# Paged latent attention of a decoder step: cache pages held as 64 partitions with turned rotary keys, and another order of TensorE's steps

## The reference

```python
past_ckv = cache_ckv[page_table].reshape(bd, -1, MLA_KV_RANK)   # 256 wide
past_kr = cache_krope[page_table].reshape(bd, -1, MLA_ROPE)     # 64 wide
s = (einsum('bqhr,bkr->bhqk', q_abs, ckv) + einsum('bqhd,bkd->bhqk', q_rope, kr)) * scale
s = where(k_pos <= q_pos, s, -inf)
o = einsum('bhqk,bkr->bqhr', softmax(s), ckv)
```

## Time and profile before

| what | value |
|---|---|
| time of three runs, median (lowest to highest) | 1618.31 us (1614.09 to 1619.07) |
| span of the profiled execution | 1614.3 us |
| TensorE busy (matmul, weight load) | 1531.1 us (95%), 1364.3 us (85%) |
| DVE, ACT, POOL busy | 821.2, 508.0, 674.4 us |
| first page transposes to last values | about 948 to 1122 us |

### The profile page before, as it was taken

One profiled execution on the slowest core, in us unless ns is written; L12 is line 12 of the kernel. 1 busy time (PEld: TensorE's weight loads), 2 busy tenths in 40 slices (PEclk: granted clock), 3 DMA queues, 4 the chain that ended last, 5 costly groups with the idle time before them and its releaser, 6 DMA issues.

```text
span 1614.3 us, 31112 instructions
## 1 busy us (share of the span) xinstructions
PE 1531.1 (95%) x11688; PEld 1364.3 (85%) x11688; DVE 821.2 (51%) x1212; ACT 508.0 (31%) x864; POOL 674.4 (42%) x558
## 2 busy tenths in 40 slices
PE   7999999979999999998899999999979999999996
PEld 7999645969999999997796556665969999999996
DVE  4721375476565663224647654443476665563224
ACT  5322340243222223113421444443243222223211
POOL 3343200346665564344332024441346665564333
PEclk9999997979999999998999999999989999999998
DMA  4222203212222223223121059982212222223221
GB/s 150 80 79 81 116 14 136 95 35 91 80 89 91 84 85 108 89 89 133 54 88 56 1 160 286 286 260 68 76 35 91 82 87 91 88 81 108 90 93 57
DMA packets 56215, 159.89 MB, mean 99 GB/s; under 512 B 7793, under 2 KB 26226, under 8 KB 54850
## 3 DMA queue, kind: packets, MB, share of 16 engines
q1 hardware_dynamic: 49986, 137.77, 25.7%
q0 software_dynamic: 6144, 20.98, 4.3%
HBM read 150.68 MB, written 8.05 MB: 98 GB/s over the span
## 4 chain that ended last, share of the span: by engine, by line
PE 84%; DVE 7%; issue 5%; ACT 2%; POOL 2%; POOLq 0%; ACTq 0%; DVEq 0%
PE lin L1510 61%; PE lin L1898 3%; PE px L1974 2%; PE px L1938 2%; DVE tb L1155 2%; POOL w_l L518 1%; PE lin L1869 1%; PE px L1886 1%; PE px L1942 1%; PE px L1906 1%; PE lin L1868 1%; DVE sq L1205 1%; DVE xg_l L979 1%; PE px L1575 1%; PE lin L1851 1%
## 5 line engine op out<-in xcount | busy, mean ns | idle before, releaser
L518 POOL TENSOR_TENSOR w_l<-w_raw,w_h 128x1024 fp32r<-128x1024 f32 (+1 forms) x142 | 384.7, 2710 | 380.9 <-ACT w_h L611 263.1
L1510 PE MATMUL lin<-xg_h,w_h 128*128 128x272 f32 x2112 | 459.3, 296 | 40.9 <-DVE xg_l L979 30.7
L1510 PE MATMUL lin<-xg_l,w_h 128*128 128x272 f32 x2112 | 447.4, 289 | 0.0
L1510 PE MATMUL lin<-xg_h,w_l 128*128 128x272 f32 x2112 | 446.8, 289 | 0.0
L1510 PEld LDWEIGHTS lin<-xg_h,w_h 128*128 128x128 f32 x2112 | 337.6, 190 | 51.0 <-DVE xg_l L979 24.8
L1510 PEld LDWEIGHTS lin<-xg_l,w_h 128*128 128x128 f32 x2112 | 340.1, 190 | 0.3
L1510 PEld LDWEIGHTS lin<-xg_h,w_l 128*128 128x128 f32 x2112 | 336.9, 190 | 0.0
L618 ACT ACTIVATE w_h<-w_raw 128x1024 fp32r<-128x1024 f32 (+1 forms) x104 | 117.3, 1128 | 233.3 <-PE lin L1510 233.3
L611 ACT ACTIVATE w_h<-w_raw 128x1024 fp32r<-128x1024 f32 (+2 forms) x71 | 77.9, 1099 | 241.5 <-PE lin L1510 223.4
L513 POOL TENSOR_TENSOR w_l<-w_raw,w_h 128x1024 fp32r<-128x1024 f32 (+2 forms) x33 | 83.9, 2543 | 166.3 <-ACT w_h L611 166.3
L1510 PE MATMUL lin<-a_h,w_h 128*128 128x272 f32 x704 | 150.4, 290 | 0.0
(11 more groups left out here) (307 smaller groups left out, 1978.7 us busy)
## 6 DMA issues: line engine op xcount, KB each, us to landing
w_raw<-w SPq DMA_DIRECT2D x139, 512.0 KB, 3.7
w_raw<-w SPq DMA_DIRECT2D x32, 704.0 KB, 4.0
pages<-cache SPq DMA_DIRECT2D x128, 160.0 KB, 3.7
pages<-cache POOLq DMA_DIRECT2D x128, 160.0 KB, 3.7
St<-state SPq DMA_DIRECT2D x4, 1024.0 KB, 7.7
gla_s<-St SPq DMA_DIRECT2D x4, 1024.0 KB, 3.9
w_raw<-w SPq DMA_DIRECT2D x4, 576.0 KB, 3.7
x<-x_t SPq DMA_DIRECT2D x4, 544.0 KB, 6.3
```

What stands on the lines that cost most here:

```text
L518: g.tensor_tensor(w_l[:, p % 2, 0:n], w_raw[:, p % 2, 0:n], w_h[:, p % 2, 0:n].bitcast(F32), ALU.subtract).then_inc(w_lo, 1)
L1510: last = mm(lin[:, 2 * out_set + half, 0:HALF], w[:, slot, (w0 + k) * P:(w0 + k + 1) * P], v[:, ch, half * HALF:(half + 1) * HALF], start= ...
```

## The change

A page in HBM is now 64 rows of 640 floats: row p holds the latent keys p and p + 64 (2 x 256) and then row p of the page's transposed rotary keys (128). A DMA writes 64 rows: SP always writes partitions 0 to 63, GpSimd 64 to 127, each with two of a group's four pages. So two pages share the 128 partitions, and their rotary keys need no transposes. The rotary scores multiply all 128 rows with `qz`, a query of which either the upper or the lower 64 rows are zero: eight matmuls of 256 columns (four runs of 64) for four of 512. There are 12 buffers instead of 14 (three of a unit's size): groups 0 to 3 wait for the prompt scores, 4 to 11 for the end of the prompt attention, later ones for the group 12 earlier. TensorE's order is groups 0 to 3, probabilities of u - 1, scores of u, values of u - 1; ACT and DVE follow it. The bytes per page stay 160 KB. The core of the diff:

```diff
@@ -210,20 +211,17 @@
...
-        qrs = at("qrs", Z + 41216, [P, NSEQ, 32])
...
+        qz = at("qz", Z + 41216, [P, 2, NSEQ, 32])
...
-        kr_t = at("kr_t", Z + 25600, [P, 2, SEQ])
...
+        pages = [at(f"pages{k}", o, [P, 8, PROW]) for k, o in enumerate((Z, Z + 67584, Z + 67584 + 4 * GROUP))]
...
@@ -313,44 +312,44 @@
...
-        def latent(g, j, lo=0, hi=KVR):
-            start = j * ROW + (ROPE if j % 2 else 0)
-            return pages[g % len(pages)][:, start + lo:start + hi]
-        def rotary_keys(g, pair):
-            return pages[g % len(pages)][:, 2 * pair * ROW + KVR:2 * pair * ROW + KVR + 2 * ROPE]
+        def latent(g, q4, lo=0, hi=KVR):
...
+        def rotary_keys(u, q4):
...
+            by_group = pages[u % len(pages)][:].rearrange("p (k e) c -> p k e c", e=2)
+            return by_group[:, :, par, 2 * KVR + 64 * key_half:2 * KVR + 64 * key_half + 64]
...
-        def load_pages(eng, which, ready):
...
+        def load_pages(eng, half, ready):
             eng.wait_ge(ids_in, 16)
-            eng.wait_ge(qa_ps, 1)
+            rows = slice(64 * half, 64 * half + 64)
             for g in range(4 * UNITS):
-                k = g % len(pages)
-                if g == 1:
+                k = g % SLOTS
+                if g == 0:
                     eng.wait_ge(sc_ps, H_M * TILES)
-                    eng.wait_ge(qr_done, 4)
-                elif g == 9:
+                    eng.wait_ge(qr_done, 6)
+                elif g == 4:
                     eng.wait_ge(ml_done, H_M)
...
-                elif g >= len(pages):
-                    eng.wait_ge(pvg_ps, g - len(pages) + 1)
-                for j in which:
-                    page = eng.value_load(page_ids[0:1, 4 * g + j:4 * g + j + 1], min_val=0, max_val=io["n_pool"] - 1)
-                    cols = slice(0, ROW) if j % 2 else slice(ROPE, ROPE + ROW)
-                    eng.dma_start(pages[k][:, j * ROW:(j + 1) * ROW], io["cache"][page, :, cols]).then_inc(ready[k], 16)
+                elif g >= SLOTS:
+                    eng.wait_ge(pvg_ps, g - SLOTS + 1)
+                for par in range(2):
+                    at_ = 4 * g + 2 * par + half
+                    page = eng.value_load(page_ids[0:1, at_:at_ + 1], min_val=0, max_val=io["n_pool"] - 1)
+                    eng.dma_start(pages[k // 4][rows, 2 * (k % 4) + par, :], io["cache"][page]).then_inc(ready[k], 16)
...
@@ -890,10 +889,6 @@
...
                 fn(k_t[:, :, 0, (g % 4) * P:(g % 4 + 1) * P], k_bank(g, 0).rearrange("p (j t) -> p j t", j=4), ACT.Copy).then_inc(ta_done, 1)
-                if g % 2:
-                    act.wait_ge(t_ps, turned(g, 3))
-                    fn(kr_t[:, :, (g % 4 - 1) * P:(g % 4 + 1) * P].rearrange("p j (e t) -> p e j t", e=2),
-                       r_bank.rearrange("p (e j t) -> p e j t", e=2, j=2), ACT.Copy).then_inc(tr_done, 1)
...
@@ -917,11 +912,10 @@
...
                     page_probs(unit_ - 1)
-                pages_turned(4 * unit_ + 1)
-                pages_turned(4 * unit_ + 2)
+                for kk in range(1, 4):
+                    pages_turned(4 * unit_ + kk)
                 if unit_:
...
-                pages_turned(4 * unit_ + 3)
             page_probs(UNITS - 1)
@@ -1367,8 +1361,9 @@
...
                 for to in range(2):
+                    v.memset(qz[ROPE * to:ROPE * to + ROPE, 1 - to], 0.0).then_inc(qr_done, 1)
                     for odd in range(2):
-                        v.tensor_copy(qrs[ROPE * to:ROPE * to + ROPE].rearrange("p b (j e t) -> p j e b t", j=4, t=TS)[:, :, odd],
+                        v.tensor_copy(qz[ROPE * to:ROPE * to + ROPE, to].rearrange("p b (j e t) -> p j e b t", j=4, t=TS)[:, :, odd],
                                       q[ROPE * odd:ROPE * odd + ROPE, 8:12, SEQ:NT].rearrange("p j (b t) -> p j b t", t=TS)).then_inc(qr_done, 1)
@@ -1431,14 +1426,13 @@
...
             for unit_ in range(UNITS):
-                for kk in range(3):
+                for kk in range(4):
                     pages_turned(4 * unit_ + kk)
...
                     new_probs_turned(unit_ - 1)
-                pages_turned(4 * unit_ + 3)
+                page_maxima(unit_)
                 if unit_:
                     page_outputs(unit_ - 1)
-                page_maxima(unit_)
             new_probs_turned(UNITS - 1)
@@ -1889,22 +1883,14 @@
             def turn_group(g):
-                for ready in (pg_ready, pg_odd):
-                    pe.wait_ge(ready[g % len(pages)], 32 * (g // len(pages) + 1))
+                for ready in (pg_low, pg_high):
+                    pe.wait_ge(ready[g % SLOTS], 32 * (g // SLOTS + 1))
                 for r in range(KC):
...
                         pe.wait_ge(ta_done if r == 0 else tv_done, g - 1)
...
                     last.then_inc(t_ps, 1)
-                if g % 2 == 0:
-                    return
-                if g > 1:
-                    pe.wait_ge(tr_done, g // 2)
-                for e in range(2):
-                    for j in range(2):
-                        last = nc.tensor.transpose(r_bank[:, (2 * e + j) * P:(2 * e + j + 1) * P], rotary_keys(g - 1 + e, j), ident[:])
-                last.then_inc(t_ps, 1)
...
@@ -1915,9 +1901,6 @@
...
-                if n == NM - 1:
-                    pe.wait_ge(pe_done, NM - 1)
-                    turn_group(0)
...
@@ -1932,26 +1915,27 @@
...
                 pe.wait_ge(tv_done, 4 * u + 4)
-                pe.wait_ge(tr_done, 2 * u + 2)
                 for r in range(KC):
-                    for j in range(4):
-                        mm(s_bank[32 * j:32 * j + 32, :], qabs[:, r, b, :], k_t[:, j, r, :], start=r == 0, stop=False,
-                           tile_position=(0, 32 * j))
-                for j in range(4):
-                    row = ROPE * (j % 2)
-                    last = mm(s_bank[32 * j:32 * j + 32, :], qrs[row:row + ROPE, b, :], kr_t[row:row + ROPE, j // 2, :],
-                              start=False, stop=True, tile_position=(row, 32 * j))
+                    for q4 in range(4):
+                        mm(s_bank[32 * q4:32 * q4 + 32, :], qabs[:, r, b, :], k_t[:, q4, r, :], start=r == 0, stop=False,
+                           tile_position=(0, 32 * q4), skip_group_check=True)
+                for half in range(2):
+                    for q4 in range(4):
+                        keys = s_bank[32 * q4:32 * q4 + 32, :].rearrange("p (k j t) -> p k j t", j=2, t=64)[:, :, half, :]
+                        last = mm(keys, qz[:, half, b, :], rotary_keys(u, q4), start=False, stop=True,
+                                  tile_position=(0, 32 * q4), skip_group_check=True)
                 if u % 2 == 0:
...
                     return
-                pe.wait_ge(o_done, u)
+                if b:
+                    pe.wait_ge(ptn_done, b)
...
                last.then_inc(qk_ps, 1)
@@ -1983,18 +1966,16 @@
             for unit_ in range(UNITS):
-                for kk in range(3):
-                    if unit_ or kk:
-                        turn_group(4 * unit_ + kk)
+                for kk in range(4):
+                    turn_group(4 * unit_ + kk)
                 if unit_:
                     turn_page_probs(unit_ - 1)
-                turn_group(4 * unit_ + 3)
+                else:
+                    pe.wait_ge(ml_done, H_M)
+                    pe.wait_ge(qr_done, 6)
+                score_unit(unit_)
                 if unit_:
                     page_values(unit_ - 1)
-                else:
-                    pe.wait_ge(ml_done, H_M)
-                    pe.wait_ge(qr_done, 4)
-                score_unit(unit_)
             turn_page_probs(UNITS - 1)
@@ -2160,7 +2141,8 @@
...
-    out["cache"] = np.concatenate([a["cache_krope"], a["cache_ckv"], a["cache_krope"]], axis=2)
+    halves_of_keys = a["cache_ckv"].reshape(-1, 2, P // 2, KVR).transpose(0, 2, 1, 3).reshape(-1, P // 2, 2 * KVR)
+    out["cache"] = np.concatenate([halves_of_keys, a["cache_krope"].transpose(0, 2, 1)], axis=2)
...
```

More of the change, by code:

```diff
@@ L49 @@
 SLOT = FC // 2 * P
-GROUP = 4 * 4 * ROW
+PROW = 2 * KVR + P
+GROUP = 4 * 2 * PROW
 PCOL = {}
@@ L220, in trunk_program @@
         nm = at("nm", Z + 46592, [P, NS])
-        kr_t = at("kr_t", Z + 25600, [P, 2, SEQ])
[L222 to L226, removed]
+        p_t = at("p_t", Z + 49536, [P, 5, P])
+        pages = [at(f"pages{k}", o, [P, 8, PROW]) for k, o in enumerate((Z, Z + 67584, Z + 67584 + 4 * GROUP))]
         k_t = at("k_t", hi_off, [P, 4, KC, SEQ])
@@ L284, in trunk_program @@
         ids_in = sem("ids_in")
[L285 to L288, removed]
+        SLOTS = 4 * len(pages)
+        pg_low = [sem(f"pg_low{k}") for k in range(SLOTS)]
+        pg_high = [sem(f"pg_high{k}") for k in range(SLOTS)]
+        t_ps, ta_done, tv_done, qk_ps, sm_done, ex_done, scale_done, pts_ps, pts_done, ptn_done, pvg_ps, o_done = (
+            sem(n) for n in ("t_ps", "ta_done", "tv_done", "qk_ps", "sm_done", "ex_done", "scale_done", "pts_ps",
```

(29 more changed lines are left out.)

15 lines of the change are left out of this document (8 added, 7 removed).

## The result

| | before | after |
|---|---|---|
| time, median of 4 runs each (lowest to highest) | 1616.71 us (1614.09 to 1619.07) | 1633.16 us (1630.83 to 1635.75) |
| span of the profiled execution | 1614.3 us | 1634.1 us |

The change makes the kernel slower: the ratio is 1.0109, 95% interval 1.0085 to 1.0133. The forecast was 1609.7 us, faster; rival B, late pages because of the half-height page stream, came true in kind. The two profiled executions differ by 19.8 us, the medians by 16.5.

What follows compares the result with a forecast made beforehand. TensorE was taken to bound the kernel, page stream close behind. -8.0 (steady units) + 2.2 + 0.5 (start) - 3.3 (end) = -8.6 us off the median 1618.31 gave 1609.7 us; own range 1604 to 1613, high end with rival B 1641.

Steps and rivals of the forecast that it cites:

- rival B: Page stage: the half-height page stream is too slow, making the kernel slower, 1638 us at 230 GB/s; chance 0.38.
- part 4: Page stream: loads keep up, issued 1.14 us apart, 9.1 us per unit against 9.6 needed.
- the upper: Page stream: DMA engines keep their rate with 64-row writes, 307 to 322 GB/s, rather than 153.
- the margin of 0.7 us: Page ring of 12: 13.6 us until a freed group is wanted, 12.9 us to issue eight loads and land.
- its marks: Page stage: TensorE waiting for pages in every unit, share near 1 under 258 GB/s, landings well over 4 us.
- part 6: End of page stage: unit 14's values fill TensorE's idle hole and the clock stays up; 3.3 us saved.
- break-even: Page stage: the kernel gains nothing at 10.14 us per unit or 258 GB/s.
- Parts 1 to 3: Steady page units: no rotary transposes, new scores, new order; 9.28 us odd, 9.90 even, 8.0 us saved.
- part 3: Page units, new order: TensorE waits about 0.5 us per unit before scores, 0.35 more in even units for ACT.
- Part 5: Start of page stage: late loads cost unit 1 2.2 us, and two memsets of `qz` cost 0.5.
- The memsets: Two of `qz` ahead of the first probabilities: between 0 and 0.9 us for both, taken as 0.5 lost.
- the limit named: After the page stage: TensorE would next wait for GpSimd's `w_l`, so only about 1.4 us of faster values count.

Runs made afterwards that it cites:

- run 2: The kernel before with only the change's page DMAs of 64 rows of 2560 bytes; 1630.11 us, ratio 1.008.
- run 6: The kernel before with page DMAs writing 64 partitions in two runs of 1280 bytes each; 1641.03 us, ratio 1.0147.
- run 5: The change with its DMAs dealt so that both queues write the same 64 partitions at about the same time; 1646.08 us, ratio 1.0165.
- run 1: The change with pages packed as 128 rows of 320 floats, order and ring of 12 kept; 1614.93 us, ratio 0.998.
- run 4: The change with the last unit's values ahead of the scores on TensorE, freeing buffers earlier; 1635.13 us, ratio 1.0106.
- run 11: run 1 with the old order of steps back on TensorE, ACT and DVE; 1612.75 us, ratio 0.9962.
- run 9: run 1 with group 0 filled early and turned before the last prompt probabilities, groups 4 to 6 loaded earlier; 1609.27 us, ratio 0.9949.
- run 12: run 9 and run 11 put together: 128-row pages, mended start, old order of steps; 1606.1 us, ratio 0.9929.
- run 10: The change, 64-row pages kept, with the mended start of run 9 alone; 1629.46 us, ratio 1.0077.
- before_ring12: The kernel before with 12 group buffers in its ring instead of 14; 1618.44 us, ratio 0.9997.

## Why the prediction was wrong

**Step that failed: part 4.** "I take the upper, because each DMA moves the same bytes in half as many, longer rows, and the two queues write different halves at the same time." The upper was 307 to 322 GB/s; the runs show 249 at a share of 1.01. Both reasons were real: long rows gave 271 instead of 235 (runs 2 and 6), different halves 249 instead of 234 (the change and run 5). They don't undo that 64 partitions are written. Landing was 4.9 us for my 3.8, so the margin of 0.7 us (13.6 against 9.1 + 3.8) became a lack of 0.4. A price was missed too: I kept SP at or below GpSimd's pace without a row for its 64-row form, whose instruction grew to 0.47 us; with SP's loads about 1.23 us apart (three in 2.93 us from 999.79) eight take 9.8, and the lack is 1.2. Page waits of 8.7 us from unit 2 on came of it. Run 1 shows that the shape is needed for them, run 4 that the late release is too: the step that failed is this margin, by the terms of landing, issue and rate. How much each of the three costs isn't parted. Nor does 249 GB/s stand as the most that this form can give: GpSimd stood 25.4 us in 13 waits for a free buffer, and run 4 had units at 257 GB/s without a wait for pages.

Rival B had the mechanism and its marks; its chance of 0.38 was too low. Its formula takes off all 3.3 us of part 6, of which 1.9 are won ahead of the last scores, so its break-even is 10.02 us per unit and 262 GB/s, not 10.14 and 258. With 10.5 us per unit (2.62 MB at 249 GB/s) it gives 944.9 + 168 + 3.8 + 4.8 - 1112.93 - 1.4 + 0.5, 8 us slower. That the measured 1633 lies near B's 1638 is luck: the start and the program's end make up most of it. The Trainium skill, page SBUF — State Buffer, section "Door 1: The DMA port swizzle", warned in the right direction; its 218 GB/s for 64 rows were too low for this stream, which reached 249 with the queues on both halves and 234 with both dealt the same one. Its 6% for a second DMA on the other half (section "Can I just issue two DMAs to hit both halves?") is against a single DMA; our 6% is against two queues on the same half, so the trace doesn't test it. The only evidence against the page's rule was an argument, no row.

**Parts 1 to 3 were right.** 9.32 and 10.02 us in run 1 for 9.28 and 9.90; scores with rotary 2.57 for 2.63, so four runs of 64 columns stream like 256; waits before the scores 0.44 and 0.33 for about 0.5, ACT's 0.23 for 0.35. No run shows part 3's 0.05 us for the semaphore: in run 1 DVE's copy ends at 989.78 and the scores start at 989.93, 0.15 later. The gain was there to be had: from unit 2's start to the start of the last scores run 1 needs 131.9 us for 139.0 before, 7.1 of the 9.9 forecast there, with 1.9 of the rest in two page waits. The change did not get it, since its pages came late. What part 3 didn't ask is whether the new order is worth its wait: run 11 shows that it costs 0.8 us per pair, and runs 9 and 12 that it costs 3.2 us in all.

**Part 5 was mis-sized.** 2.2 + 0.5 was forecast, 10.2 came. The memsets took 0.27 us each, inside my 0 to 0.9. Left out was the clock: it was priced in part 6 from the hole in the earlier trace rows, while here the same kind of hole was opened by moving group 0. It cost 2.2 us on the last values (4.63 for 2.42), 0.7 on the four groups (4.38 for 3.71 in run 1's unit 3), and again 1.4 on unit 1's scores (3.36 for 1.92) after the page waits. Those were 4.9 us in unit 1, where I had one of 2.6. Run 9 shows the start as a cost of its own, 5.7 us; run 10's 3.7 point the same way without being clear of noise.

**Part 6 was right.** The values of the unit before fill the hole, the clock stays (TensorE stands 0.98 and 0.58 us, and the window from 1120 to 1140 us shows 1.00) and the output projection then waits 0.68 us for GpSimd's `w_l`, the limit named. From the end of the last scores to the first L1504 it took 7.65 us for 8.86: 1.2 saved for the 1.4 forecast. The other 1.9 of part 6's 3.3 are the values that no longer stand ahead of the last scores.

**Not in the prediction at all:** 7.2 us at the program's end, 44% of the difference of the medians. No row of before could show it; the term "what lies outside the stage" was silently zero.

Still open: why the same form of DMA moved 271 GB/s in run 2 and 249 in the change. The sources differ as well (2560 bytes of each 3072 there, one contiguous block here); that was not tried apart. In run 2 TensorE was busy in every microsecond, so 271 may not be the most there either. Nor do the runs show why the drain grows, only with what; and no run has 64-row pages with both the early release and a covered `p_t` copy, which would show the rate that this form can hold.

## What to carry to other kernels

A stream that runs with the DMA engines this busy (0.92 here) should not be reshaped on an argument: in these runs the number of partitions that a DMA writes is part of its price, and equal bytes are no equal time. Keep the tiles that a compute change wants and the shape that the transfers want apart: the same removal of transposes, with pages as 128 rows, beat the change by 18 us and, with the start mended and the old order, the kernel before by 12. When one run leaves the time as it was, look at the waits before a theory is dropped: in run 4 one wait had gone and another had come. When a step is moved away from a gap, ask what the clock does in the gap, and test a new order of steps alone, since one that rides along with a gain can hide a cost of its own.

## What the runs showed of the hardware that was not expected

- GpSimd's closing DRAIN took 12.3 us in all six kernels in which GpSimd issued 128 DMAs of 64 rows of 2560 bytes, and 4.8 to 5.1 us in all others, also with 64 partitions and runs of 1280 bytes. Its DMAs had landed 500 us earlier.
- SP's DMA instruction took 0.333 us for 128 rows of 1280 bytes, 0.469 for 64 of 2560, 0.537 for 64 partitions with two runs each; GpSimd's 0.536, 0.516 and 0.587.
- From 970 to 1070 us the kernels with 64-row DMAs show DMA shares of 0.95 to 1.07 at 234 to 271 GB/s, those with 128-row DMAs alone 0.88 to 0.93 at 271 to 289. At 271 GB/s one stood at 1.03 (before_rows64), another at 0.88 (before_ring12). The share alone would not have told which was better off.
- 64-row DMAs on one queue slow the other queue's 128-row DMAs: landings of 11.3 and 7.2 us for 3.7.
